# Prompt's matrix memory in a pipeline of four heads, q, k and gates in one stage, and keys of the sample's attention in column tiles

## The reference

```python
# layer 1: mLSTM, chunkwise; q, k, v, o, input gate, forget gate from one projection
q, k, v, o, ig, fg = _split(xn @ w_in, ODD_SIZES)          # 8 heads, DQK 64, DV 128
ig = ig + b_i;  lf = log_sigmoid(fg + b_f)
def step(carry, xs):                                       # over chunks
    c, n, m = carry
    b = cumsum(fc);  a = b + m
    d = where(causal, b[l] - b[s] + ic[s], -inf)
    mj = maximum(a, max(d));  s = (qc @ kc.T) * exp(d - mj);  aw = exp(a - mj)
    num = s @ vc + aw * (c @ qc);  den = sum(s) + aw * (n . qc)
    h = num / maximum(abs(den), exp(-mj))
    g = b_last - b + ic;  m_new = maximum(b_last + m, max(g))
    c_new = exp(b_last + m - m_new) * c + sum_s exp(g - m_new) * vc kc^T   # n_new likewise
```

```python
# layer 0, sample: each query attends over 256 keys picked out of 4096 paged keys and its new ones
s = einsum(q, k_sel); s = where(valid, s, -inf); p = softmax(s); o = p @ v_sel
```

## Time and profile before

| | |
|---|---|
| median of 3 runs | 4011.34 us (4008.31 to 4024.57) |
| the profiled execution | 4013.81 us, its span 4012.0 us |
| TensorE busy (matmul) | 3463.9 us, 86% of the span |
| VectorE, ScalarE busy | 1845.7 us (46%), 1414.1 us (35%) |
| mean granted TensorE clock | 0.912 of full speed |

### The profile page before, as it was taken

How to read it: one execution, slowest core, us unless ns; L and a number is a source line. 1 busy time by engine, 2 the same in 40 slices (tenths; PEclk the granted TensorE clock), 3 DMA queues, 4 the chain that set the end, 5 groups by cost and what they waited for, 6 DMA issues and landing times. The chain is left out here.

```text
span 4012.0 us, 44253 instructions
## 1 busy us (share of the span) xinstructions
PE 3463.9 (86%) x17367; PEld 2737.3 (68%) x17367; DVE 1845.7 (46%) x3229; ACT 1414.1 (35%) x2349; POOL 122.4 (3%) x137
## 2 busy tenths in 40 slices
PE   5979994987888799999997998686598799999997
PEld 4744652544776699899785765475377589889885
DVE  3566998611334444444544310342633444444443
ACT  4452112632334433433444310221333443333443
POOL 0002110023000000000000000000000000000000
PEclk9989997999999899999998999655699999999998
DMA  2013112036112333333441100001203143343343
GB/s 78 25 28 111 48 56 83 1 131 210 48 49 94 119 125 123 122 126 126 142 132 42 39 31 22 1 1 24 69 1 116 41 159 120 112 133 123 126 157 115
DMA packets 225440, 341.78 MB, mean 85 GB/s; under 512 B 33733, under 2 KB 162349, under 8 KB 225234
## 3 DMA queue, kind: packets, MB, share of 16 engines
q1 hardware_dynamic: 213458, 297.00, 22.8%
q0 software_dynamic: 11776, 41.95, 3.2%
HBM read 328.43 MB, written 10.19 MB: 84 GB/s over the span
## 5 line engine op out<-in xcount | busy, mean ns | idle before, releaser
L198 PE MATMUL ps<-s_mlp_xl,s_mlp_w1h 128*128 128x384 f32 (+1 forms) x1536 | 498.7, 325 | 10.7 <-DVE s_mlp_xl L603 10.7
L585 DVE TENSOR_TENSOR s_mlp_w2l<-s_mlp_w2b,s_mlp_w2h 128x1024 fp32r<-128x1024 f32 x192 | 235.1, 1225 | 581.9 <-ACT s_mlp_w2h L471 581.9
L200 PE MATMUL ps<-s_mlp_xh,s_mlp_w1h 128*128 128x384 f32 (+1 forms) x1536 | 495.4, 323 | 0.0
L199 PE MATMUL ps<-s_mlp_xh,s_mlp_w1l 128*128 128x384 f32 (+1 forms) x1536 | 494.9, 322 | 0.0
L198 PE MATMUL ps<-s_mlp_w2l,s_mlp_hh 128*128 128x512 f32 x1024 | 404.3, 395 | 20.4 <-DVE s_mlp_hl L622 16.2
L471 ACT CAST s_mlp_w2h<-s_mlp_w2b 128x1024 fp32r<-128x1024 f32 x192 | 201.5, 1050 | 585.9 <-PE ps L200 585.7
L199 PE MATMUL ps<-s_mlp_w2h,s_mlp_hl 128*128 128x512 f32 x1024 | 402.3, 393 | 0.0
L200 PE MATMUL ps<-s_mlp_w2h,s_mlp_hh 128*128 128x512 f32 x1024 | 402.1, 393 | 0.0
L198 PEld LDWEIGHTS ps<-s_mlp_xl,s_mlp_w1h 128*128 128x128 f32 x1536 | 289.4, 188 | 42.5 <-issue 36.3
L199 PEld LDWEIGHTS ps<-s_mlp_xh,s_mlp_w1l 128*128 128x128 f32 x1536 | 289.3, 188 | 6.2
L200 PEld LDWEIGHTS ps<-s_mlp_xh,s_mlp_w1h 128*128 128x128 f32 x1536 | 289.2, 188 | 0.0
(11 more groups left out here) (503 smaller groups left out, 6051.6 us busy)
## 6 DMA issues: line engine op xcount, KB each, us to landing
s_mlp_w1b<-w_ff SPq DMA_DIRECT2D x96, 1024.0 KB, 6.1
s_mlp_w2b<-w_ff SPq DMA_DIRECT2D x96, 1024.0 KB, 8.3
x<-x_prompt SPq DMA_DIRECT2D x2, 4096.0 KB, 13.0
x_kb<-cache_mem_k SPq DMA_DIRECT2D x16, 512.0 KB, 7.5
x_vb<-cache_mem_v SPq DMA_DIRECT2D x2, 4096.0 KB, 20.4
s_orows_raw<-w_in_odd SPq DMA_DIRECT2D x32, 256.0 KB, 3.5
s_convsel_w<-w_in_even SPq DMA_DIRECT2D x12, 512.0 KB, 3.7
ev_mixT<-w_in_even SPq DMA_DIRECT2D x16, 256.0 KB, 3.3
```

The lines of the kernel that those rows point to most:

```text
L198: nc.tensor.matmul(out, ah, bl, start=first, stop=False, skip_group_check=True)
L199: nc.tensor.matmul(out, al, bh, start=False, stop=False, skip_group_check=True)
L200: return nc.tensor.matmul(out, ah, bh, start=False, stop=last, skip_group_check=True)
L585: nc.vector.tensor_tensor(w2l[:, s % RING], w2b[:, c % 3, s % FC, :], w2h.bitcast(F32)[:, s % RING], ALU.subtract).then_inc(low2, 1)
```

## The change

In `sattend` the keys of a set are turned into eight `kT` buffers, copied by ScalarE (even units) and VectorE (odd ones). The scores of a set's four sequences follow one another, column tile by column tile. The exponential is made in five pieces of a half.

q, k and gates share `stage_qk_gates`. The gate products have the tokens on the partitions; then everything runs with (chunk, head) on 72 partitions and 128 columns. TensorE's small work for the gates stands between the q/k units 2, 8, 11 and 15; the bias, mask and state loads are queued by SP behind the first weight piece. `stage_turned` and `stage_gates` go.

In `mlstm` the mask is added by TensorE (a product with the identity in fp32r), and the stabilisers are subtracted there too, from a stationary made of one column of the identity. ScalarE takes the exponential straight from PSUM. Buffers are doubled, TensorE makes the stabilisers, carried part and scores of unit i + 1 before the part within unit i, and VectorE divides one unit late. The update of the state is four products in two column tiles, so that VectorE updates the state in two instructions of 128 rows instead of four of 64. GpSimd gates the keys. `state_C` is loaded in this stage, and no longer in the next.

```diff
 stage_sample_attend
-        kT = S.sb("kT", [P, 2, SEQ])
+        kT = S.sb("kT", [P, 8, SEQ])
...
-            def score(i):
-                hf, g, b4 = units[i]
+            def score(n):
+                hf, g = divmod(n, 4)
                 bk = 4 + 2 * ((5 * hf + g) % 2)
-                pe.wait_ge(k_kept, i + 1)
+                for q in range(2):
+                    pe.wait_ge(k_kept[q], 2 * n + 2)
                 for a in range(2):
-                    ins = nc.tensor.matmul(G.ps[32 * b4:32 * b4 + R, bk + a, :], qb[:, 4 * hf + b4, :],
-                                           kT[:, i % 2, a * 512:(a + 1) * 512], start=False, stop=True, tile_position=(0, 32 * b4))
+                    for b4 in range(4):
+                        ins = nc.tensor.matmul(G.ps[32 * b4:32 * b4 + R, bk + a, :], qb[:, 4 * hf + b4, :],
+                                               kT[:, 4 * (n % 2) + b4, a * 512:(a + 1) * 512], start=False, stop=True,
+                                               tile_position=(0, 32 * b4))
+                ins.then_inc(product, 1)
...
+            for i in range(4):
+                turn(i)
+            for n in range(8):
+                if n < 7:
+                    turn(4 * n + 4)
+                    turn(4 * n + 5)
+                bias(n // 4, n % 4)
+                score(n)
+                if n % 4 == 3:
+                    score_new(n // 4)
+                if n < 7:
+                    turn(4 * n + 6)
+                    turn(4 * n + 7)
...
 stage_qk_gates, TensorE
+            pe.wait_ge(side_in, 64)
+            for t, r in enumerate(ROWS):
+                for k in range(KD):
+                    ins = nc.tensor.matmul(G.ps[0:r, 6, t * 16:(t + 1) * 16], G.xnT[:, k, t * P:t * P + r], wg[:, k, :],
+                                           start=(k == 0), stop=(k == KD - 1))
+            ins.then_inc(gated, 1)
+            for i, (n, c) in enumerate(units):
...
+                if i >= 6:
+                    pe.wait_ge(kept, i - 5)
...
+                if i == A1:
+                    pe.wait_ge(biased, 2)
...
+                elif i == A2:
+                    pe.wait_ge(ended, 1)
...
+                elif i == A3:
+                    pe.wait_ge(begun, 1)
...
+                elif i == A4:
+                    pe.wait_ge(exps, 3)
...
 stage_mlstm, TensorE
+            def stabilise(i):
+                c, f = units[i]
+                if i >= 2:
+                    pe.wait_ge(exped, i - 1)
+                nc.tensor.matmul(G.ps[:, i % 2, :], identR[:], later[:].rearrange("p j t -> p (j t)"), start=True, stop=False,
+                                 skip_group_check=True)
                 for j in range(4):
-                    nc.tensor.matmul(G.ps[:, 0, j * P:(j + 1) * P], selh[:, 4 * f + j, :], O.M[:, tok], start=True, stop=True).then_inc(stab, 1)
+                    row = H * c + 4 * f + j
+                    ins = nc.tensor.matmul(G.ps[:, i % 2, j * P:(j + 1) * P], bc(G.ident[0:NR, row:row + 1], [NR, P]),
+                                           O.M[0:NR, :], start=False, stop=(j == 3), skip_group_check=True)
+                ins.then_inc(stab, 1)
...
+            def update(i):
...
+                for j in range(4):
+                    o = 64 * (j % 2)
+                    ins = nc.tensor.matmul(G.ps[o:o + 64, 7, (j // 2) * VE:(j // 2 + 1) * VE], kg[:, i % 2, j, :],
+                                           O.v[:, c, 4 * f + j, :], start=True, stop=True, tile_position=(0, o))
...
+            for i in range(N):
+                if i + 1 < N:
+                    stabilise(i + 1)
+                update(i)
+                if i + 1 < N:
+                    carry(i + 1)
+                    score(i + 1)
+                within(i)
...
 stage_mlstm, ScalarE and GpSimd
+                act.wait_ge(stab, i + 1)
+                if i >= 2:
+                    act.wait_ge(weighted, i - 1)
+                for j in range(4):
+                    ins = nc.scalar.activation(wt[:, i % 2, j, :], G.ps[:, i % 2, j * P:(j + 1) * P], ACT.Exp, scale=-1.0,
+                                               bias=O.cols[:, c, GI, 4 * f + j:4 * f + j + 1])
...
+                if i >= 2:
+                    pool.wait_ge(updated, i - 1)
+                nc.gpsimd.tensor_tensor(kg[:, i % 2], O.krow[:, c, 4 * f * HD:(4 * f + 4) * HD].rearrange("p (j e) -> p j e", j=4),
+                                        bc(O.cols[:, c, GW, 4 * f:4 * f + 4].unsqueeze(2), [P, 4, HD]), ALU.mult).then_inc(kgated, 1)
```

More of the change, by code:

```diff
@@ L1760, in _ @@
             pe.wait_ge(q_made, 1)
[L1761 to L1774, removed]
+            for i in range(4):
[11 more added lines that the diff above has]
+                    turn(4 * n + 7)
             def turn_weights(hf, g):
                 i = N + 6 * hf + g
-                pe.wait_ge(exped, hf + 1)
+                pe.wait_ge(exped, 5 * hf + g + 1)
                 bank_free(i)
@@ L2459, in _ @@
-            dve.wait_ge(logged, 1)
-            chain(nc.vector.scalar_tensor_tensor(out=lf, in0=x, scalar=0.0, in1=a, op0=ALU.min, op1=ALU.subtract))
-            for c in range(NT):
-                cs = slice(c * P, (c + 1) * P)
-                chain.add(nc.vector.tensor_tensor_scan(b[:, cs], lf[:, cs], G.zeros8[:], 0.0, ALU.add, ALU.add))
-            bs, ls = groups(b, True), groups(lf, True)
+            for v in (ig, x, b):
+                chain.add(nc.vector.memset(v[:], 0.0))
+            chain.add(nc.vector.memset(starts[:, 0, 0:H], 0.0))
@@ L2465, in _ @@
+            chain(nc.vector.scalar_tensor_tensor(out=lf[:], in0=x[:], scalar=0.0, in1=a[:], op0=ALU.min, op1=ALU.subtract))
+            bs, ls, Ms, gs = (by_batch(v) for v in (b, lf, M, gi))
+            chain.add(nc.vector.tensor_tensor_scan(b[0:R, :], lf[0:R, :], G.zeros8[:], 0.0, ALU.add, ALU.add))
             chain(nc.vector.tensor_copy(bs[:, :, 0:1], ls[:, :, 0:1]))
@@ new lines, in _ @@
+            dve.wait_ge(gturned, 2)
+            chain(nc.vector.tensor_copy(ends[:], G.ps[0:1, 6, 0:2 * R].rearrange("p (j r) -> p j r", j=2)))
+            for h in range(H):
+                last, total, out = (v.rearrange("p (c h) -> p c h", h=H)[:, :, h] for v in (ends[:, 0, :], ends[:, 1, :], after[:]))
+                chain.add(nc.vector.tensor_tensor_scan(out, last, total, 0.0, ALU.max, ALU.add))
+            chain.wait()
+            chain(nc.vector.tensor_copy(starts[:, 0, H:R], after[:, 0:R - H]))
@@ L2501, in _ @@
-            chain(nc.vector.tensor_copy(O.dbh[:], G.ps[0:DB, 5, 0:H]))
+            chain.add(nc.vector.tensor_copy(O.cols[:], G.ps[:, 6, 0:4 * R].rearrange("p (j t h) -> p t j h", j=4, t=NT)))
+            chain.add(nc.vector.tensor_copy(O.cols_s[:], G.ps[0:NS, 6, 4 * R:4 * R + 4 * H].rearrange("p (j h) -> p j h", j=4)))
+            dve.wait_ge(turned, 2)
+            for q in range(2):
+                rows = slice(64 * q, 64 * q + 64)
+                chain.add(nc.vector.tensor_copy(O.dcol[rows], G.ps[rows, 7, 0:R].rearrange("p (c a q) -> p q a c", c=NT, q=2)[:, q]))
@@ L2504, in stage_krows @@
+            chain(nc.vector.tensor_copy(O.dbh[:], G.ps[0:DB, 7, R:R + H]))
 def stage_krows(nc, G, O):
```

465 lines of the change are left out of this document (256 added, 209 removed).

## The result

The changed kernel takes 3856.7 us (median of four runs, 3844.8 to 3871.4) where the kernel before takes 4012.3: ratio 0.9609, 95% interval 0.9569 to 0.9649. The profiled execution took 3859.09 us, with a span of 3857.1. The span fell by 155 us against 4012.0, where the forecast had 114.5.

A forecast was written before the change was run, and what follows sets the result against it. TensorE was taken to bound the key half, transfers the value half, and the loop to stay at the lower clock. 4012.0 + 1.8 - 114.5 (-41, -45, -17, -12, +0.5) - 2.5 gave 3897 us, own range 3878 to 3912.

The forecast's parts named there:

- wide range: Whole kernel: 8 in 10 of the outcomes, rivals included, lie in 3832 to 3918 us.
- main forecast: Whole kernel: 3897 us, own range 3878 to 3912, chance 0.45.
- rival of the full clock: `mlstm` loop: runs at full clock once its gaps are closed, saving 80 us in place of 17, so 3834; chance 0.30.
- Keys: Key half of `sattend`: 70.6 us in place of 111.5, -41 us (bounds -30 to -45).
- W: Key half of `sattend`: TensorE's work a set, with turns, bias, scores and waits on copies, 8.2 us.
- L: Key half of `sattend`: a set's gather with the start of its issue, 8.6 us, upper bound 10.7.
- gathers' rival: Key half of `sattend`: gathers bound it, with a period of 10.7 us, 16 us more, so 3913; chance 0.12.
- q, k and gates: Merged stage from odd rows to key rows: 159.2 us in place of 204.0, -45 us (bounds -34 to -54).
- Loop: `mlstm`, 16 units: 9.4 us a unit in place of 10.49 at the lower clock, -17 us (bounds -5 to -25).
- The rival "half way": `mlstm` loop: gets half way to the full clock, so 3865 us; no chance of its own given.
- Sample's memory: Start of the sample's memory stage: TensorE's 12.3 us wait for `state_C` goes, -12 us.
- The slow rival: `mlstm` stabilisers: stationary read with step 0 costs more; at 1.1 us more a pass the kernel takes 4037; chance 0.02.

The follow-up runs named there:

- `state_C` late: Changed kernel with the load of `state_C` back at the head of the sample's stage, as before the change; 3866.3 us.
- order of scores: Changed kernel with a set's scores sent sample by sample, four passes in a row to one column tile; 3846.6 us.
- early gates: Changed kernel with a semaphore of its own for the gates' weights, so TensorE's first gate product waits for these alone; 3846.9 us.
- gathers by the quarter: Changed kernel with each of a set's four gathers sent once its own quarter of the buffer has been turned; 3845.6 us.
- the kernel with the filled wait: Changed kernel with four unread products of 512 columns on TensorE while it waits for the mask before the loop; 3828.5 us.
- the one with 128 rows: Changed kernel with the stabilisers' products over 128 rows instead of 64, zeros in the unused rows; 3827.8 us.
- the kernel before with 128 rows: Kernel before the change, stabilisers' stationary padded with zeros from 8 to 128 rows and moving operand read over 128 rows; 3976.7 us.

## Why the prediction was right, and where not

3856.7 lies in the wide range (3832 to 3918), and 21 us below the main forecast's own range (3878 to 3912). Of the 40 us by which the fall of the span exceeds 114.5, the loop has 37. Three terms held; the loop's clock, which the text called the choice that decides, was taken wrong for half of the loop. That the number fell in the wide range is owed to the rival of the full clock, and to the loop's getting there only half way.

**Keys, right, in part by luck.** -41 forecast, -41.5 measured. W is 7.9, not 8.2: from 892.55 to 900.43 four turns take 3.9 for 4.2, the scores 1.85 for 2.0, the bias 1.81 for 1.71, and the wait for a copy is the 0.3 that was forecast. L is 9.8, not 8.6. The period is then (7.9 + 9.8) / 2 = 8.85 by the forecast's own formula, and 8.7 as measured, for 8.4. So the six middle periods took 52.2 us for 50.4, with TensorE waiting 0.5 to 2.2 us for a gather at four of the six sets, and only what lies before and after them, 17.8 for 20.2, brought the sum back. The gathers' rival had L at 10.7, nearer the 9.8 than the forecast was, but its period of 10.7 did not come.

**q, k and gates, right.** -45 and -46.3. Start 8.96 for 8.6, gate products 28.45 for 29.2: 0.198 a pass of 16 columns at a clock of 0.50, where the 0.203 came from passes of four columns, at 0.54 and not at the lower level throughout. All that follows took 120.3 for 121.4, and TensorE shows no wait for the chain of the gates between the units, as forecast.

**Loop, order of work right, clock wrong in its second half.** At the lower clock the sum had 9.4 a unit and the trace 8.79. By steps: mask and within 2.44 in place of 2.55, stabilisers 2.01 for 2.07, update 1.05 for 1.3 (its lower bound: the two column tiles overlap fully), carry and scores 3.29 for 3.2 (the trace of before has 3.29 for them too, from 2634.76 and not 2634.83), and the steps between, 0.25, don't exist. That is worth 9 us. The rest is the sentence "So I take the lower level as likelier": it failed for the second half of the loop. Seven periods at or near the full level took 34.8 us where the lower level would have taken 61.5. The rival "half way" had 3865, and with the shorter unit it comes near the measured time. What I argued from, that 89% busy did not hold the clock, was a true row with the wrong reading: the loop of before rose to 0.97 with its waits untouched once the stabilisers went over 128 rows. The other argument, that most passes are still of 64 rows, is of the right kind, but such passes held the full level once it was there (38.50 of 40.40 us busy at 1.00).

**When it rises differs.** In five kernels whose TensorE does the same in the loop, the number of periods at 8.8 us before the clock rose was seven (changed kernel), six (`state_C` late), five (order of scores), five (early gates) and two (gathers by the quarter), and their loops took 109.9, 106.4, 102.3, 102.3 and 90.0 us: 4 us a period, as 8.79 - 4.85 says. The changed kernel's four runs spread over 26.6 us, the kernel with the filled wait over 4.8 and the one with 128 rows over 8.3. Loops here are counted to the end of the last part within, 0.5 us less than in the table. What makes the clock rise in mid-loop stays open, and whether those edits elsewhere set the moment; the two groups of runs of the kernel before with 128 rows speak for chance from run to run. Shown is that filling the wait, or 128 rows in the changed kernel, narrows the spread and takes all runs (at most 3833.8) below the changed kernel's lowest (3844.8).

**Sample's memory, right.** -12 forecast, -14.3 seen from loop to first transpose, 13.2 by undoing it.

**The slow rival** (a stationary read with step 0) did not come: the stabilisers cost 2.01.

## What to carry over

Look up the granted clock at the entry of a loop, not only its mean: here, with a wait of 3.6 us ahead of it, the loop ran 70 of its 110 us at the lower level, and a few products that nobody reads gave 28 us back. Price a stage that ran at the lower level at both, and try zeros in the unused rows of small products: here they took no time, and the higher level came in all runs of the new form and in seven of ten of the old one. A pass costs its pitch, not its row's duration, and buffers that are freed by the quarter are worth trying wherever a DMA waits for the whole.

## What the runs showed that was not expected

Padding a product from 8 or 64 rows to 128 lowered the period, from 4.85 to 4.66 us at full clock and from 10.49 to 10.19 at half. A loop at the same busy share held either level of the clock for long: 0.51 with TensorE 99% busy, and 1.00 at 95% in the same loop. Sixteen passes of 512 columns over four column tiles took 1.92 us in one order and 1.94 in the other, although in the second each tile's four passes came one behind the other in the program. Were no pass to start before the one ahead of it in the program, and a tile's passes to start 0.43 us apart, the pitch of the earlier trace rows, the last would start 12 x 0.43 = 5.2 us after the first (an estimate), and all of them ended within 1.94. So passes of different tiles seem to have run side by side out of the program's order; which start belongs to which tile, the trace doesn't show. The Trainium skill, page "TensorE: Matmul & The Clock Gate", section "The mechanism", has the matmuls start strictly in order; this run speaks against that, without showing it. On GpSimd the product of 128x256 elements with two inputs took 0.61 us, within the 0.6 to 0.8 of the prediction.
